# Attention stage of a decoder block: VectorE's order of choice, products and residual reads, the norm's affine part moved to VectorE, tile turns at lag 13

## What is computed

```python
w = p[:, :, 0] - lam * p[:, :, 1]                  # two softmaxes per head, 4 heads
o = rms_norm(einsum(w, v), subln_g) * (1 - lambda_init)
mix = concat([att, ssd]) @ w_out
x = layer_norm(alpha * x + mix, ln1_g, ln1_b)      # residual read, statistics, affine part
q = x @ w_q                                        # expert choice: 8 heads, two halves each
s1, i1 = top_k(scores[..., 0, :], 16); s2, i2 = top_k(scores[..., 1, :], 16)
top_s, pos = top_k(s1[:, None] + s2[None, :], 16); ids = ...
act = gelu(dot(x, u_tab[ids])) * gates             # the "products" are these dots
x = layer_norm(alpha * x + act @ v_tab[ids], ln2_g, ln2_b)
```

## Time and profile before

| | us |
|---|---|
| median of 3 runs | 3322.46 |
| lowest and highest run | 3312.59, 3324.89 |
| span of the profiled execution | 3313.3 |
| TensorE busy | 2784.6 |
| VectorE busy | 1887.9 |
| GpSimd busy | 1483.6 |
| ScalarE busy | 596.6 |
| attention block, start to its last product | about 418 to 882 |

### The profile page before, as it was taken

How to read it: one execution, slowest core, us unless ns; L and a number is a source line. 1 busy time by engine, 2 the same in 40 slices (tenths; PEclk the granted TensorE clock), 3 DMA queues, 4 the chain that set the end, 5 groups by cost and what they waited for, 6 DMA issues and landing times.

```text
span 3313.3 us, 32683 instructions
## 1 busy us (share of the span) xinstructions
PE 2784.6 (84%) x10171; PEld 1374.6 (41%) x10171; DVE 1887.9 (57%) x4634; ACT 596.6 (18%) x1288; POOL 1483.6 (45%) x1348
## 2 busy tenths in 40 slices
PE   8999979755356888757589999999999999899996
PEld 3455545433123555424334444444444444344442
DVE  3335444688698888678845655546666544444113
ACT  1321033321004888500000000000000000000000
POOL 0011001345644443344565666566665566565452
PEclk9999979877677899878799999999999999999998
DMA  3100021355877999898999999999999999999995
GB/s 119 39 26 26 26 74 67 128 188 208 290 275 277 387 385 387 320 358 314 328 395 387 397 404 405 368 403 401 404 404 376 364 398 407 387 398 384 369 372 204
DMA packets 307579, 981.57 MB, mean 296 GB/s; under 512 B 29904, under 2 KB 57680, under 8 KB 306640
## 3 DMA queue, kind: packets, MB, share of 16 engines
q0 software_dynamic: 184320, 671.17, 53.1%
q1 hardware_dynamic: 120464, 307.85, 24.7%
q10 hardware_dynamic: 2624, 0.46, 0.1%
HBM read 941.63 MB, written 37.75 MB: 296 GB/s over the span
## 4 chain that ended last, share of the span: by engine, by line
PE 30%; issue 13%; POOL 11%; DMA 10%; DVE 6%; ACT 2%; ACTq 1%; DVEq 1%; POOLq 0%
PE part L1806 10%; PE hid L1787 9%; DMA v_ring<-in_peer_v_dram,ids_t 8%; POOL u_ring L1725 7%; PE acc L1844 6%; POOL v_ring L1739 4%; PE turn_ps L1779 4%; DVE u_ring L2122 2%; DMA u_ring<-in_peer_u_dram,ids_u 1%; ACT dense_sums L1884 1%; PE part L1815 1%; ACTq L1885 1%; ACT dense_sums L1886 1%; DMA room<-in_peer_v_dram 1%; DVE dense_sums L2130 1%
## 5 line engine op out<-in xcount | busy, mean ns | idle before, releaser
L2122 DVE CUSTOM_DVE_ANT_0 u_ring<-u_ring,x_rows_in 128x1024 f32<-128x1024 f32 x560 | 676.7, 1225 | 510.0 <-DMA u_ring<-in_peer_u_dram,ids_u 497.3
L1725 POOL DMA_INDIRECT u_ring<-in_peer_u_dram,ids_u x560 | 628.4, 1122 | 501.7 <-DVE dots L2122 357.7
L1739 POOL DMA_INDIRECT v_ring<-in_peer_v_dram,ids_t x560 | 593.7, 1060 | 479.2 <-PE acc L1844 334.0
L1806 PE MATMUL part<-room 128*128 128x512 f32 x1536 | 693.2, 601 | 88.5 <-DVE room L2098 76.4
L1787 PE MATMUL hid<-x1t_dense,room 128*128 128x384 f32 x2048 | 699.9, 495 | 6.3 <-DMA room<-in_peer_ut_dram 4.8
L1787 PEld LDWEIGHTS hid<-x1t_dense,room 128*128 128x128 f32 x2048 | 385.7, 193 | 340.3 <-issue 101.0
L1806 PEld LDWEIGHTS part<-room 128*128 128x128 f32 x1536 | 292.1, 192 | 448.2 <-issue 338.0
L1844 PE MATMUL acc<-v_ring,line 128*32 128x512 f32 x2240 | 292.6, 643 | 67.7 <-DMA v_ring<-in_peer_v_dram,ids_t 65.4
L1922 ACT ACTIVATE room<-hid 128x384 f32<-128x384 f32 x128 | 62.9, 491 | 1465.8 <-PE hid L1787 1465.8
L2108 DVE TENSOR_TENSOR dense_sums<-dense_sums,part 128x512 f32<-128x512 f32 x186 | 125.9, 685 | 270.9 <-PE part L1806 270.7
L412 PE MATMUL bank<-w_ring,xt 128*128 128x512 f32 x512 | 225.1, 592 | 2.7 <-issue 2.7
(11 more groups left out here) (320 smaller groups left out, 2640.9 us busy)
## 6 DMA issues: line engine op xcount, KB each, us to landing
wq_pair<-in_peer_wq_dram SPq DMA_DIRECT2D x32, 2048.0 KB, 14.6
room<-in_peer_ut_dram SPq DMA_DIRECT2D x128, 512.0 KB, 7.4
room<-in_peer_v_dram SPq DMA_DIRECT2D x128, 512.0 KB, 9.8
gate_grid<-room SPq DMA_DIRECT2D x6, 4096.0 KB, 14.0
room<-gate_grid SPq DMA_DIRECT2D x32, 768.0 KB, 18.4
w_ring<-in_w_in_dram SPq DMA_DIRECT2D x5, 2048.0 KB, 8.0
u_ring<-in_peer_u_dram,ids_u POOLq DMA_INDIRECT x560, 9.7
v_ring<-in_peer_v_dram,ids_t POOLq DMA_INDIRECT x560, 10.4
```

Source lines behind the costliest of these rows:

```text
L1725: pool.indirect_dma_start(u_ring[:, n % U_RING, :], None, peer_u, bass.IndirectOffsetOnAxis(ap=ids_u[:, q, k:k + 1], axis=0))\
L1739: pool.indirect_dma_start(row, None, peer_v, bass.IndirectOffsetOnAxis(ap=ids_t[:, q % 2, token:token + 1], axis=0))\
L1806: last = mm.matmul(part[k % 3][:], weights[:, n % 2, i, d * P:(d + 1) * P], vd[:, slot, half * 512:(half + 1) * 512], start=(i == 0), stop ...
L2122: vec.tensor_tensor_reduce(u_ring[:, n % U_RING, :], u_ring[:, n % U_RING, :], x1[:, q % 2, :], 1.0, 0.0, ALU.mult, ALU.add, dots[:, q % 2 ...
```

## The change

VectorE takes, in each step, choice and products ahead of the residual read and the normalisation. VectorE does the affine part for every tile (before, only for the last) and makes x1_first itself. GpSimd loses the affine part and takes the variance's power after the step's asks. TensorE and ScalarE turn and copy the normalised tile one step later, and earlier within that step: behind the scores, and behind the exps. Two semaphores fall away and the loop is one step longer.

```diff
-        last_step = items - 1 + 12
+        last_step = items - 1 + 13
...
@@ -896,23 +894,6 @@
                     if tail(n, 7) is not None:
                         pool.wait_ge(av_ready, 1).then_inc(av_ready, -1)
                         pool.tensor_tensor(ar[:], av[:], half_neg[:], ALU.pow).then_inc(ar_ready, 1)
-                    if tail(n, 10) is not None:
-                        pool.wait_ge(var_ready, 1).then_inc(var_ready, -1)
-                        pool.tensor_tensor(rstd[:], var[:], half_neg[:, 0:1], ALU.pow).then_inc(rstd_ready, 1)
-                    if (t := tail(n, 11)) is not None:
-                        tile = x1[:, t % 2, :]
-                        if t == 0:
-                            pool.wait_ge(norm_in, 48)
-                        pool.wait_ge(normed, 1).then_inc(normed, -1)
-                        if t < NT - 1:
-                            pool.tensor_tensor(tile, tile, g1[:], ALU.mult).then_inc(step, 1)
-                            pool.wait_ge(step, 1).then_inc(step, -1)
-                            pool.tensor_tensor(tile, tile, b1[:], ALU.add).then_inc(step, 1)
-                            pool.wait_ge(step, 1).then_inc(step, -1)
-                        pool.sem_inc(x1_ready, 1)
-                        pool.sem_inc(x1_turn, 1)
-                        if t == 0:
-                            pool.tensor_copy(x1_first[:], tile).then_inc(x1_first_ready, 1)
                     for k in rows_asked(n):
                         if k % TOPK == 0:
                             pool.wait_ge(ids_ready, 1).then_inc(ids_ready, -1)
@@ -923,6 +904,9 @@
                         pool.indirect_dma_start(row_at(k), None, peer_u,
                                                 bass.IndirectOffsetOnAxis(ap=ids_first[:, k:k + 1], axis=0))\
                             .then_inc(rows_landed[landed(k)], 16)
+                    if tail(n, 10) is not None:
+                        pool.wait_ge(var_ready, 1).then_inc(var_ready, -1)
+                        pool.tensor_tensor(rstd[:], var[:], half_neg[:, 0:1], ALU.pow).then_inc(rstd_ready, 1)
...
@@ -965,6 +949,14 @@
                 for n in range(last_step + 1):
                     if n < items:
                         scores(n)
+                    if tail(n, 13) is not None:
+                        pe.wait_ge(x1_turn, 1).then_inc(x1_turn, -1)
+                        for h2 in range(2):
+                            pe.wait_ge(t_free[h2], 1).then_inc(t_free[h2], -1)
+                            for i in range(4):
+                                at = (4 * h2 + i) * P
+                                last = mm.transpose(TP[h2][:, i * P:(i + 1) * P], x1[:, tail(n, 13) % 2, at:at + P], ident[:])
+                            last.then_inc(t_done[h2], 1)
@@ -1012,14 +1004,6 @@
...
-                    if tail(n, 12) is not None:
...
@@ -1035,6 +1019,18 @@
+                    if tail(n, 13) is not None:
+                        act.wait_ge(x1t_landed, 16).then_inc(x1t_landed, -16)
+                        for h2 in range(2):
+                            act.wait_ge(t_done[h2], 1).then_inc(t_done[h2], -1)
+                            act_.activation(x1t[:, 4 * h2:4 * h2 + 4, :].rearrange("p i n -> p (i n)"), TP[h2][:], ACT.Copy)
+                            if n == 13:
+                                act_.activation(x1t_first[:, 4 * h2:4 * h2 + 4, :].rearrange("p i n -> p (i n)"), TP[h2][:], ACT.Copy)
+                            act.drain().then_inc(t_free[h2], 1)
+                        if n == 13:
+                            act.sem_inc(x1t_first_ready, 1)
+                        act.sem_inc(x1t_ready, 1)
+                        act.sem_inc(x1_free, 1)
                     if 2 <= n < items + 2:
...
-                    if tail(n, 12) is not None:
...
@@ -1132,6 +1116,21 @@
                             vec.scalar_tensor_tensor(out=part, in0=part, scalar=ar[:, h:h + 1], in1=sub_g[:],
                                                      op0=ALU.mult, op1=ALU.mult)
                         dve.drain().then_inc(att_ready, 1)
+                    for which in range(2):
+                        if (g := choice(n, 5 + which)) is not None:
+                            at = slice(which * DKEY, (which + 1) * DKEY)
+                            head = 2 * g + which
+                            dve.wait_ge(pair_for_dve, 1).then_inc(pair_for_dve, -1)
+                            choose_experts(vec, dve, b, sc_pair[:, at], top_first[:, head * TOPK:(head + 1) * TOPK],
+                                           ids_first[:, head * TOPK:(head + 1) * TOPK], pair_seen).then_inc(ids_ready, 1)
+                            if which:
+                                dve.wait_ge(pair_seen, 2).then_inc(pair_seen, -2)
+                                dve.sem_inc(pair_free, 1)
+                    for k in products(n):
+                        row = row_at(k)
+                        dve.wait_ge(rows_landed[landed(k)], 16 * sum(landed(i) == landed(k) for i in range(k + 1)))
+                        vec.tensor_tensor_reduce(row, row, x1_first[:], 1.0, 0.0, ALU.mult, ALU.add,
+                                                 dots_first[:, k:k + 1]).then_inc(rows_free, 1)
                     if (t := tail(n, 10)) is not None:
                         dve.wait_ge(xtile_in, 16).then_inc(xtile_in, -16)
                         for half in range(2):
...
                         dve.wait_ge(rstd_ready, 1).then_inc(rstd_ready, -1)
                         vec.tensor_scalar(tile, tile, mv[:, 0:1], rstd[:, 0:1], ALU.subtract, ALU.mult)
                         dve.drain()
-                        if t == NT - 1:
-                            vec.tensor_tensor(tile, tile, g1[:], ALU.mult)
+                        vec.tensor_tensor(tile, tile, g1[:], ALU.mult)
+                        dve.drain()
+                        vec.tensor_tensor(tile, tile, b1[:], ALU.add)
+                        dve.drain().then_inc(x1_ready, 1)
+                        dve.sem_inc(x1_turn, 1)
+                        if t == 0:
+                            vec.tensor_copy(x1_first[:], tile)
                             dve.drain()
-                            vec.tensor_tensor(tile, tile, b1[:], ALU.add)
-                            dve.drain()
-                        dve.sem_inc(normed, 1)
-                    for which in range(2):
...
-                    for k in products(n):
-                        if k == 0:
-                            dve.wait_ge(x1_first_ready, 1)
...
```

More of the change, by code:

```diff
@@ L786, in build_mixer @@
         rstd_ready = handshake("rstd_ready1")
-        normed = sem("normed")
-        x1_first_ready = sem("x1_first_ready")
         x1_ready = handshake("x1_ready")
@@ L1014, in _ @@
                             last.then_inc(op_done, 1)
-                    if tail(n, 12) is not None:
-                        pe.wait_ge(x1_turn, 1).then_inc(x1_turn, -1)
-                        for h2 in range(2):
-                            pe.wait_ge(t_free[h2], 1).then_inc(t_free[h2], -1)
-                            for i in range(4):
-                                at = (4 * h2 + i) * P
-                                last = mm.transpose(TP[h2][:, i * P:(i + 1) * P], x1[:, tail(n, 12) % 2, at:at + P], ident[:])
-                            last.then_inc(t_done[h2], 1)
             @block.scalar
@@ L1063, in _ @@
                         act.sem_inc(mix_ready, 1)
-                    if tail(n, 12) is not None:
-                        act.wait_ge(x1t_landed, 16).then_inc(x1t_landed, -16)
-                        for h2 in range(2):
-                            act.wait_ge(t_done[h2], 1).then_inc(t_done[h2], -1)
-                            act_.activation(x1t[:, 4 * h2:4 * h2 + 4, :].rearrange("p i n -> p (i n)"), TP[h2][:], ACT.Copy)
-                            if n == 12:
-                                act_.activation(x1t_first[:, 4 * h2:4 * h2 + 4, :].rearrange("p i n -> p (i n)"), TP[h2][:], ACT.Copy)
-                            act.drain().then_inc(t_free[h2], 1)
-                        if n == 12:
-                            act.sem_inc(x1t_first_ready, 1)
-                        act.sem_inc(x1t_ready, 1)
-                        act.sem_inc(x1_free, 1)
                     if choice(n, 0) is not None:
@@ L1154, in _ @@
                         dve.drain()
-                        if t == NT - 1:
-                            vec.tensor_tensor(tile, tile, g1[:], ALU.mult)
-                            dve.drain()
-                            vec.tensor_tensor(tile, tile, b1[:], ALU.add)
-                            dve.drain()
-                        dve.sem_inc(normed, 1)
-                    for which in range(2):
-                        if (g := choice(n, 5 + which)) is not None:
-                            at = slice(which * DKEY, (which + 1) * DKEY)
-                            head = 2 * g + which
-                            dve.wait_ge(pair_for_dve, 1).then_inc(pair_for_dve, -1)
```

(15 more changed lines are left out.)

## The result

The changed kernel ran in 3295.92 us (median of 10 runs, 3287.45 to 3302.82). The kernel before, run beside it, had 3312.18 (median of 10, 3303.87 to 3324.89). Ratio 0.9944, 95% interval 0.9929 to 0.9959. The profiled execution has a span of 3289.0 us and its own time is 3290.78, so 1.8 us lie around a span.

The account below looks back on a forecast made before the run. The prediction took the block's end, set by when VectorE finishes its last product, to move the whole time one for one. Its terms summed to -18.0 us, against the median 3322.46 giving 3304.5, eight in ten from 3296 to 3318.

Parts of the forecast that it names:

- Part 1: Early steps, tile turns at lag 13 instead of 12: a loss, +4.2 us at tile 0 and +0.8 at tile 1.
- Part 2: Steps 22, 26, 30: products ahead of the residual read fit in VectorE's wait for the projection; -2.7, -3.2, -4.5 us.
- Part 3: Steps 23, 27, 31: affine part off GpSimd ends stretched products, VectorE pays 2.7 us itself; -2.0, -1.6, -1.6 us.
- Part 4: Tail from step 34 on: fewer stretched operations, no late row, a shorter projection wait in step 38; -7.4 us.
- hand-off dearer: Rival: the longer chain of exps, copies and turns costs 3 us more at each of tiles 1 to 3; 3313, chance 0.13.
- more gain: Rival: step 30's projection takes 14 us instead of 16.45 and the first hand-off costs half; say 3298, chance 0.12.
- Slower: clock: Rival: TensorE stays at 1.2 GHz through the projections of steps 26, 30 and 38, 42 us in all; 3346, chance 0.07.

Follow-up runs that it names:

- g2: The changed kernel plus 5 unread matrix products in each of two TensorE gaps, steps 12 and 13; ratio to the kernel before 0.9922.
- a: The kernel before with only the normalised tile's turn and copies moved one step later (lag 13 instead of 12); ratio to the kernel before 1.0009.
- b: The kernel before with only the affine part moved from GpSimd to VectorE, in its old place; ratio to the kernel before 0.9999.
- g: The changed kernel plus 8 unread matrix products in each of two TensorE gaps, steps 12 and 13; ratio to the kernel before 0.9936.
- c: The kernel before with VectorE's new order, affine part still on GpSimd but behind the step's asks; ratio to the kernel before 0.9970.
- f: The changed kernel with turns back at lag 12 and the affine part on GpSimd for tiles 0 to 2; ratio to the kernel before 0.9922.
- k: f plus 4 unread matrix products ahead of each output projection of steps 26 and 30; ratio to the kernel before 0.9919.

## Why the prediction came out as it did

**The time.** 3304.5 with a range of 3296 to 3318 was forecast, 3295.92 came: 0.1 below the range. The edit's effect was right (3304.5 / 3322.46 = 0.9946 against 0.9944 measured, -18.0 against -18.2 at the last product as profiled and -18.0 by the ruler). What failed is the last step of the sum, "Against the median: 3304.5", which takes 3322.46, a median of three, for the time of the kernel before. These three are among the ten runs of the result, whose median is 3312.18, 10.3 lower; the other seven lie between 3303.87 and 3317.25, and in the later comparisons the kernel before had medians of 3310.96 to 3315.67. The prediction had the 3313.3 of the span and the 3312.59 of the lowest run beside it. The range allowed for -10 about the median in words and then ended at 3296, 8.5 below the forecast; 3312.18 - 18.0 = 3294.2 would have been the forecast, 1.7 from what came.

**Part 1**, by the ruler. Tile 0: +4.2 forecast, +6.6 measured at scores(14) (29.68 against 23.07). The term that was mis-sized is TensorE's, which the prediction left as it was: scores(13) had taken 2.31 and the products with v 1.95, and they took 1.05 and 1.27 more (2.3 of the 2.4 missing). g2, with its granted clock of 1.00 instead of 0.50 and 0.59, shows that the level is the cause. The copy into x1_first took 0.70 (0.8 taken). Tile 1 and 2: +0.8 forecast, and +0.8 is what maxima(22) are later than maxima(14) (6.46 against 5.65); both directions came, -2.4 at maxima(17) and +3.5 at (18). The second half of the projection of step 22 is read 6.8 later than before, as the forecast had it (+5.0 and +1.9), but VectorE itself is 6.5 later by then, so only 0.3 of it is the projection's own. Maxima(23) +2.5 against +2.3.

**Part 2.** Step 22 gave -3.9 (-2.7 forecast), step 26 -4.5 (-3.2): by the ruler the projection began 0.6 later than before and took the same 13.97, so its second half was ready 0.6 later and not 1.5; VectorE read it without a wait, and waited 0.59 and 0.27 us for rows. Step 30 gave -5.3 (-4.5): the projection took 15.67 instead of 16.45.

**Part 3.** Step 23 gave -1.9 (-2.0), step 27 -1.5 (-1.6). The Trainium skill, SBUF — State Buffer, "Who interferes with whom", as the prediction read it, would have the asks at 0.93 us throughout. Behind the change an ask that begins beside two products still takes up to 1.99 (the median of 60 asks is 1.10), so the row was the better guide.

**Part 4.** Behind maxima(31) the forecast is -9.0 (-1.6 of step 31 and the tail's -7.4), measured -7.2. The row wait went from 3.81 to 0.54, but the wait for the second half stayed at 3.37 (3.56 before) where about 2 was expected. The projection of step 38, which the forecast has at 14.2, took 15.49, at a granted clock of 0.90; it began 0.6 earlier than forecast and so ended 0.7 later, while VectorE's products were done 0.6 earlier. It takes 13.97 in before, behind 1.12 us of idle time, and in a, behind 1.33, and 15.49 to 16.24 in the twelve other profiles, behind 1.12 in each. No run shows what lowers the level there.

The misses (+1.5 in part 1 at the maxima, since scores(14) themselves took 1.77 instead of 2.75, then -1.2, -1.3, -0.8 in part 2, +1.8 in the tail, and small ones) nearly cancel. That -18.0 was forecast and -18.0 came by the ruler is luck in good part; the terms were off by up to 1.8. Of the rivals, "hand-off dearer" happened at tile 0 alone, "more gain" in step 30 in part; no row was over 0.8 us late. "Slower: clock" happened in small at the projection of step 38, +1.5; no other was longer than before, and that of step 30 was 0.8 shorter.

What the prediction didn't say is that parts 2 and 3 need each other. It sums them as if each stood alone; for the whole change this did no harm, but b was expected at -7.5 for that reason.

## What to carry to other kernels

Work that waits for nothing goes ahead of the read that waits; and a wide GpSimd operation costs twice, in what VectorE does beside it and in the asks behind it. Here neither the new order alone (-11.1) nor the affine part alone (-1.6) gave what both did (-21.6). Count edits from an event inside the stage, and take the level of the time from the span and the lowest run as well as from a median of three. A hand-off that makes TensorE idle can be paid again in the instructions behind it; in these runs unread matrix products that fit the gap took that back, and products that overran it gave the gain away (g).

## What the runs showed of the hardware

- A VectorE instruction of one column is stretched like a wide one: 2.70 us instead of 0.22 beside GpSimd's 2.35 us multiplication (c); the two end within 0.02 us of each other.
- A 128x1024 fp32 copy on VectorE, SBUF to SBUF, takes 0.70 us, where a two-input operation of that shape takes 1.23.
- The same 32 matrix product records took 15.67 us behind 3.80 us of idle time and 13.97 behind 3.60 us of fillers and 0.38 idle; a filler of 512 columns shows as two records of 0.44 us. The idle time just ahead does not set the length by itself: 13.97 behind 3.26 us (b), 15.53 behind 2.55 (c).
- The projection of step 38 takes 13.97 us (before) or 15.49 to 16.24 (all others but a) behind the same 1.12 us of idle time, with granted clocks of 1.00 (before) and 0.90 (after).
- TensorE's level at a given place differs between executions of programs that are equal up to there: the turn of tile 0 took 1.94 us in f and 1.06 in k, both behind 2.54 idle, and scores(13) behind it 2.37 and 2.89.
